# Another order of the attention stage in a two-layer encoder kernel

## The chip, the cores and the metric

One core of a Trainium2 chip. The metric is the device time of the whole program in microseconds (us), here the median of three runs. Engines are called TensorE (PE in the profile, its weight loads PEld), VectorE (DVE), ScalarE (ACT), GpSimd (POOL) and SyncE (SP).

## The reference

Two layers on x of 512 tokens by 1024 features, all in float32. Layer 0 mixes tokens by differential attention, layer 1 by a pooling mixer; each is followed by an MLP.

```python
h = rmsnorm(x, norm_mix[0])
q, k, v = split(h @ w_qkv)                 # 8 heads, two 64-wide maps each, v 128 wide
q = partial_rope(rmsnorm(q, q_gain)); k = partial_rope(rmsnorm(k, k_gain))
s = q @ k.T / sqrt(64)                     # 2 maps per head, 512 x 512
p = softmax(s); a = p[0] - lam * p[1]      # one learned lam
o = rmsnorm(a @ v, sub_gain) * (1 - lambda_init)
x = x + o @ w_o
x = x + square(relu(rmsnorm(x, norm_mlp[0]) @ w1[0])) @ w2[0]   # 1024 -> 4096 -> 1024
# layer 1: centred window means (2, 4, 8, 16) minus token, a matrix per group, then the same MLP
```

## The kernel before

Each float32 operand of a matmul is kept as a high and a low part (two tensors of the type fp32r), and a product is three matmuls: high by high, high by low, low by high (`three`). ScalarE makes the high part with a copy, VectorE the low part with a subtraction, so every tile that TensorE leaves in a PSUM bank is read by both, ScalarE first.

The attention has 8 heads of 4 query tiles, 32 tiles, treated as 16 pairs; pair j holds tiles 2j and 2j+1. The work is written out as steps j = 0 to 15 (and some more to drain), and each engine has its own program that follows the steps. Nothing is scheduled at run time: an engine does what is next in its program, and waits there for semaphores.

What TensorE does in step j: the scores of tiles 2j and 2j+1 (`scores`, into PSUM pairs 0 and 1, each a map per bank); the product of values and turned map of pair j-2 (`values`, bank 6); the transposes of the mixed maps of pair j-1 (`turn("map", ...)`, banks 4 and 5); then fillers, and side turns. A filler is work that doesn't belong to the pair, done in banks 6 and 7: fillers 0 to 7 project q and k of heads 4 to 7, 8 to 11 project v of these heads (24 matmuls each, in two parts of 12), and 12 to 19 are parts of the output projection w_o (6 to 18 matmuls). The table `FILL` says in which step and slot a filler's parts go. Side turns (`SIDE`) are transposes of q and k of the next head (even steps up to 12) and of a head's finished output (odd steps from 5), through banks 4 and 5, which they share with the map turns; `BACK` is the transpose of a head's values back to tokens (odd steps from 3, bank 4).

The others, for a tile or a pair: VectorE takes the negative maxima of a tile's scores (`maxima`, L1348); ScalarE the exponentials with their sums (`exps`, L969, two per tile); VectorE the reciprocal and the factor (`mix_root` L1353, `mix_factor` L1358) and `combine` (L1365), which subtracts lambda times the second map: this is called the mixing here. TensorE turns the map, ScalarE copies its high part (`keep_turn`, L913), VectorE its low part (`turn_lo`, L1310). A filler of q or k goes through ScalarE's copy and square (`qk_copy`, L894 and L897), VectorE's sum (`qk_sum`, L1272), GpSimd's root and product (`qk_root`, L690 and L696) and VectorE's rotation (`qk_norm`, L1292 to L1295). Side turns have the same two copies (L918, L1313). `o_stats` (L1371 to L1376) sums a head's squares. Weight slabs 4 to 8 (four pieces each) are split inside the steps by ScalarE (`split_hi`) and VectorE (`split_lo`) as the table `SPLIT` says; slab 8 is the first of the MLP's.

The order of the copies is each engine's own. Before, VectorE in step j does: the mixing of pair j-1, side turns of j-1, a v filler's low part, both maxima of j, the low halves of the map turns, sums of squares, weight pieces, q/k norms, head statistics. ScalarE: side copies and back copy of j-1, late fillers of j-1, exponentials of 2j, the map copies, exponentials of 2j+1, fillers, weight pieces. TensorE waits for the low half of a bank's last tile before it turns another into it (`turn`), and for the square of a filler's tile before it writes its bank again (`filler`).

After the steps come the rest of w_o, the sum with x per 128 features (`add_wo`, L1412), its squares and their sums on GpSimd (L733), the norm, and the MLP of layer 0.

## Time and profile before

| | us |
|---|---|
| median of three runs (990.47, 993.78, 994.23) | 993.78 |
| the profiled execution | 994.28 |
| its span, first to last instruction | 992.5 |
| TensorE busy in it | 967.6 |
| attention stage, steps 0 to 15 | 79.5 to 260.2 |

The profile shows one execution. Each engine's row of the timeline has the start and the length of an instruction, its line, its output and inputs; a bracket behind it gives the time that the engine was idle just before, and whose result ended that. Neighbouring equal instructions are drawn together (x8) and their lengths overlap, so the cost of one is the distance from its start to the next. The granted clock is the share of full speed that TensorE's clock was given in a stretch.

### The profile page before, as it was taken

The page shows a single profiled execution, that of the slowest core. Times are in us where ns is not written, and L with a number is a line of the kernel's source. Part 1 is how long each engine was busy: PE and PEld are TensorE (multiplying, and loading weights), DVE is VectorE, ACT ScalarE, POOL GpSimd, SP SyncE. Part 2 cuts the span into 40 slices and gives each one's busy share as a digit, 9 for nine tenths or more (in the row PEclk, how much of TensorE's full clock was granted, in tenths as well). Part 3 has the DMA queues.
Part 4 walks back from the last instruction along what each step waited for, and adds up shares of the span by engine and source line. Part 5 has one row for each costly group of instructions (what it writes and reads, how often), then busy time and mean ns, then how long its engine had stood idle before and what let it go on. Part 6 is the DMA issues. An engine that isn't in the chain of part 4 may idle for free.

```text
span 992.5 us, 12731 instructions
## 1 busy us (share of the span) xinstructions
PE 967.6 (97%) x4652; PEld 799.0 (81%) x4652; DVE 828.2 (83%) x1077; ACT 475.0 (48%) x743; POOL 351.5 (35%) x309
## 2 busy tenths in 40 slices
PE   8999898998999999999999999999999999999998
PEld 7887677877887878888888888988888888888887
DVE  5784877888566999999998888789998988989883
ACT  5645564667456452544534443575344353452520
POOL 6630333143346547385642200450431404314000
PEclk9999999999999999999999999999999999999999
DMA  7341211201140433333243232303333233322202
GB/s 260 89 126 43 86 43 43 85 1 44 43 153 34 131 108 105 108 104 109 86 124 96 79 129 82 128 1 106 107 106 106 86 111 101 122 91 85 86 0 85
DMA packets 50965, 90.12 MB, mean 91 GB/s; under 512 B 8268, under 2 KB 9560, under 8 KB 50904
## 3 DMA queue, kind: packets, MB, share of 16 engines
q1 hardware_dynamic: 45456, 89.14, 28.2%
q10 hardware_dynamic: 5448, 0.17, 0.3%
q8 instruction: 37, 0.61, 0.2%
q14 instruction: 24, 0.20, 0.1%
HBM read 87.20 MB, written 2.10 MB: 90 GB/s over the span
## 4 chain that ended last, share of the span: by engine, by line
PE 77%; DVE 13%; ACT 4%; POOL 3%; issue 2%; DMA 1%; SPq 0%; ACTq 0%; POOLq 0%; DVEq 0%
PE pair L1702 38%; PE bank L1702 36%; DVE s_nmax L1348 2%; DVE s_p L1365 1%; ACT s_p L969 1%; DVE s_w_lo L1199 1%; DVE s_aT_lo L1310 1%; POOL s_nsum L733 1%; POOL s_qk_r L690 1%; DVE s_acc L1467 1%; PE bank L1774 1%; DVE s_qkT_lo L1313 1%; ACT s_aT_hi L913 1%; DVE s_lbB_lo L1226 1%; DMA s_x_nat<-in_x 1%
## 5 line engine op out<-in xcount | busy, mean ns | idle before, releaser
L1226 DVE TENSOR_TENSOR s_lbB_lo<-s_lbB,s_b_hi 128x1024 fp32r<-128x1024 f32 x64 | 126.0, 1992 | 1.3 <-POOL s_lt L759 1.0
L759 POOL TENSOR_TENSOR s_lt<-s_lbB,s_lbB 128x1024 f32<-128x1024 f32 x14 | 34.7, 2476 | 260.4 <-PE pair L1702 162.4
L1199 DVE TENSOR_TENSOR s_w_lo<-s_raw,s_w_hi 128x1024 fp32r<-128x1024 f32 x72 | 118.9, 1675 | 3.1 <-ACT s_w_hi L838 3.1
L860 ACT ACTIVATE s_b_hi<-s_lbB 128x1024 fp32r<-128x1024 f32 x64 | 67.2, 1054 | 78.0 <-POOL s_lbB L759 35.5
L1702 PE MATMUL bank<-s_hT_hi,s_w_hi 128*128 128x512 f32 x256 | 100.2, 392 | 0.0
L1702 PE MATMUL pair<-s_hT_hi,s_w_hi 128*128 128x512 f32 x256 | 100.2, 391 | 0.0
L1702 PE MATMUL bank<-s_hT_hi,s_w_lo 128*128 128x512 f32 x256 | 99.6, 389 | 0.0
L1702 PE MATMUL bank<-s_hT_lo,s_w_hi 128*128 128x512 f32 x256 | 99.6, 389 | 0.0
L1702 PE MATMUL pair<-s_hT_hi,s_w_lo 128*128 128x512 f32 x256 | 99.6, 389 | 0.0
L1702 PE MATMUL pair<-s_hT_lo,s_w_hi 128*128 128x512 f32 x256 | 99.6, 389 | 0.0
L1058 ACT ACTIVATE s_u_raw<-s_u_raw 128x512 f32<-128x512 f32 x64 | 40.4, 632 | 114.1 <-DVE s_u_raw L1434 114.1
L838 ACT ACTIVATE s_w_hi<-s_raw 128x1024 fp32r<-128x1024 f32 x60 | 61.6, 1052 | 42.1 <-PE pair L1702 20.1
L860 ACT ACTIVATE s_b_hi<-s_lt 128x1024 fp32r<-128x1024 f32 x42 | 44.6, 1061 | 73.1 <-POOL s_lt L759 64.3
L969 ACT ACTIVATE s_p<-pair,s_nmax 128x512 f32<-128x512 f32 x64 | 43.8, 698 | 43.4 <-DVE s_nmax L1348 43.4
L1470 DVE TENSOR_TENSOR s_acc<-s_acc,bank 128x512 f32<-128x512 f32 x84 | 55.1, 678 | 6.2 <-PE bank L1702 6.2
L690 POOL TENSOR_TENSOR s_qk_r<-s_qk_v,s_minus_half 128x8 f32<-128x8 f32 x16 | 30.2, 1889 | 84.4 <-DVE s_qk_v L1273 84.4
L1470 DVE TENSOR_TENSOR s_acc<-s_acc,pair 128x512 f32<-128x512 f32 x84 | 55.1, 679 | 4.3 <-PE pair L1702 4.3
L1702 PE MATMUL bank<-s_b_hi,s_u_hi 128*128 128x512 f32 x144 | 56.6, 393 | 1.1 <-DVE s_a_lo L1458 1.1
L1702 PE MATMUL pair<-s_b_hi,s_u_hi 128*128 128x512 f32 (+1 forms) x148 | 57.4, 388 | 0.0
L1702 PEld LDWEIGHTS pair<-s_hT_hi,s_w_hi 128*128 128x128 f32 x256 | 48.1, 188 | 10.4 <-DVE s_hT_lo L1416 0.4
L1702 PEld LDWEIGHTS pair<-s_hT_lo,s_w_hi 128*128 128x128 f32 x256 | 48.1, 188 | 10.2 <-issue 0.2
L1702 PEld LDWEIGHTS bank<-s_hT_lo,s_w_hi 128*128 128x128 f32 x256 | 48.1, 188 | 10.2 <-issue 0.2
(272 smaller groups left out, 2664.0 us busy)
## 6 DMA issues: line engine op xcount, KB each, us to landing
s_raw<-in_mlp_w SPq DMA_DIRECT2D x64, 512.0 KB, 3.7
s_lbB<-in_mlp_w SPq DMA_DIRECT2D x64, 512.0 KB, 3.3
s_raw<-in_attn_w_qkv SPq DMA_DIRECT2D x24, 512.0 KB, 4.5
s_raw<-in_attn_w_o SPq DMA_DIRECT2D x8, 512.0 KB, 3.3
s_x_nat<-in_x SPq DMA_DIRECT2D x4, 512.0 KB, 7.1
out<-s_acc SPq DMA_DIRECT2D x7, 256.0 KB, 2.0
s_raw<-in_pool_w SPq DMA_DIRECT2D x4, 256.0 KB, 2.7
out<-s_acc SPq DMA_DIRECT2D x2, 128.0 KB, 1.9
```

Source lines behind the costliest of these rows:

```text
L690: root = g.tensor_tensor(qk_r[:, n % 2, :], qk_v[:, n % 2, :], minus_half[:], ALU.pow)
L733: g.tensor_tensor(nsum[:], first_sum, nsq[:, c % 4, :], ALU.add).then_inc(n_summed, 1)
L759: g.tensor_tensor(w2_raw[n][:], w2_raw[one][:], w2_raw[two][:], ALU.subtract).then_inc(t_done, 1)
L838: a.activation(w_hi[0][:, k * PIECE:(k + 1) * PIECE], raw[k][:], ACT.Copy).then_inc(w_hi_done, 1)
L860: a.activation(b_hi[home][:], w2_raw[n][:], ACT.Copy).then_inc(w2_hi_done, 1)
L969: a.activation(probs[n % 3][:, m, :], pair[n % 2][:, m, :], ACT.Exp, bias=nmax[:, n % 4, m:m + 1], accum_out=lsum[:, n, m:m + 1]).then_inc ...
L1058: a.activation(u_raw[:, f, :], u_raw[:, f, :], ACT.Square).then_inc(u_done, 1)
L1199: v.tensor_tensor(w_lo[slot][:, cols], raw[k][:], f32(w_hi[slot][:, cols]), ALU.subtract)\
L1226: v.tensor_tensor(w2_lo[n][:], w2_raw[n][:], f32(b_hi[home][:]), ALU.subtract).then_inc(w2_lo_done, 1)
L1348: v.tensor_reduce(nmax[:, n % 4, :], pair[n % 2][:], AX.X, ALU.max, negate=True).then_inc(max_done, 1)
L1470: last = v.tensor_tensor(dst, dst, src, ALU.add)
L1702: return nc.tensor.matmul(o, lhsT, rhs, start=start, stop=stop, **kw)
```

## The change

Four tables and orders are edited. A filler slot is added between the scores and the values (slot 0), so that the old slots 0 and 1 are now 1 and 2; filler 2 (step 1) and filler 5 (step 3) go into the new slot, ahead of the map turns, and of the others none follows another directly. On VectorE, the mixing of pair j moves from the start of step j+1 to step j, behind the low halves of the map turns; head statistics go ahead of those, side turns of step j and weight pieces behind the mixing. On ScalarE, side copies and the back copy move from the start of step j+1 to step j, ahead of the weight copies. The square of a q/k filler is taken from the copied tile and not from the bank, so TensorE waits for the copy only (`qk_copied`), and ScalarE waits for its own copy before the square. The last slab's pieces (slab 8) are split in steps 16 and 17 instead of 18 and 19.

```diff
-FILL = {(0, 0): ((0, 0), (0, 1)), (0, 1): ((1, 0), (1, 1)), (1, 0): ((2, 0), (2, 1)), (1, 1): ((3, 0),),
-        (2, 0): ((3, 1),), (2, 1): ((4, 0), (4, 1)), (3, 0): ((5, 0), (5, 1)), (3, 1): ((6, 0),),
-        (4, 0): ((6, 1),), (4, 1): ((7, 0), (7, 1))}
-FILL |= {(f - F_V + 5, 0): ((f, 0), (f, 1)) for f in range(F_V, F_Y)}
-FILL |= {(f - F_Y + 9, 0): ((f, 0),) for f in range(F_Y, F_END)}
+FILL = {(0, 1): ((0, 0), (0, 1)), (0, 2): ((1, 0), (1, 1)), (1, 0): ((2, 0), (2, 1)), (1, 1): ((3, 0),),
+        (2, 1): ((3, 1),), (2, 2): ((4, 0), (4, 1)), (3, 0): ((5, 0), (5, 1)), (3, 1): ((6, 0),),
+        (4, 1): ((6, 1),), (4, 2): ((7, 0), (7, 1))}
+FILL |= {(f - F_V + 5, 1): ((f, 0), (f, 1)) for f in range(F_V, F_Y)}
+FILL |= {(f - F_Y + 9, 1): ((f, 0),) for f in range(F_Y, F_END)}
...
-SPLIT = {4: (0, 0, 0, 1), 5: (2, 2, 3, 3), 6: (5, 5, 6, 6), 7: (10, 12, 13, 14), 8: (18, 18, 19, 19)}
+SPLIT = {4: (0, 0, 0, 1), 5: (2, 2, 3, 3), 6: (5, 5, 6, 6), 7: (10, 12, 13, 14), 8: (16, 16, 17, 17)}
...
-                a.activation(qs[n % 4][:], src[:], ACT.Copy, scale=in_r[:, n % NT:n % NT + 1])
+                a.activation(qs[n % 4][:], src[:], ACT.Copy, scale=in_r[:, n % NT:n % NT + 1]).then_inc(qk_copied, 1)
+                act.wait_ge(qk_copied, n + 1)
                 if n >= 3:
                     act.wait_ge(qk_v_done, n - 2)
-                a.activation(qsq[n % 3][:], src[:], ACT.Square, scale=in_r[:, n % NT:n % NT + 1])\
-                    .then_inc(qk_squared, 1)
+                a.activation(qsq[n % 3][:], qs[n % 4][:], ACT.Square).then_inc(qk_squared, 1)
...
             for j in range(END + 1):
-                for turn in SIDE.get(j - 1, ()) if j else ():
-                    keep_turn(*turn)
-                if j - 1 in BACK:
-                    keep_back(BACK[j - 1])
                 for f in range(F_END):
-                    if FILLED[f] == (j - 1, 1) or F_V <= f < F_Y and FILLED[f] == (j - 1, 0):
+                    if FILLED[f] == (j - 1, 2) or F_V <= f < F_Y and FILLED[f] == (j - 1, 1):
                         filled(f)
                 if j < PAIRS:
                     exps(2 * j)
+                for f in range(F_END):
+                    if FILLED[f] == (j, 0):
+                        filled(f)
...
                 for f in range(F_END):
-                    if FILLED[f] == (j, 0) and not F_V <= f < F_Y:
+                    if FILLED[f] == (j, 1) and not F_V <= f < F_Y:
                         filled(f)
+                for turn in SIDE.get(j, ()):
+                    keep_turn(*turn)
+                if j in BACK:
+                    keep_back(BACK[j])
...
-            for j in range(END + 2):
-                if 1 <= j <= PAIRS:
-                    mix_root(j - 1)
-                    mix_factor(j - 1)
-                    combine(2 * j - 2)
-                    combine(2 * j - 1)
-                for turn in SIDE.get(j - 1, ()) if j else ():
-                    turn_lo(*turn)
+            for j in range(END + 1):
+                if j < PAIRS:
+                    maxima(2 * j)
                 for f in range(F_V, F_Y):
-                    if FILLED[f] == (j - 1, 0):
+                    if FILLED[f] == (j - 1, 1):
                         v_lo_part(1, f - F_V, bank[FILL_BANK[f]])
                 if j < PAIRS:
-                    maxima(2 * j)
                     maxima(2 * j + 1)
+                for f in range(F_V):
+                    if FILLED[f][0] == j - 1:
+                        qk_sum(2 * NT + f)
+                if j in STATS:
+                    o_stats(STATS[j])
                 if 1 <= j <= PAIRS:
                     turn_lo("map", 2 * j - 2)
                     turn_lo("map", 2 * j - 1)
-                for f in range(F_V):
-                    if FILLED[f][0] == j - 1:
-                        qk_sum(2 * NT + f)
+                if j < PAIRS:
+                    mix_root(j)
+                    mix_factor(j)
+                    combine(2 * j)
+                    combine(2 * j + 1)
                 for s, steps in SPLIT.items():
                     for k in range(4):
                         if steps[k] + 1 == j:
                             split_lo(s, k, s % 2)
+                for turn in SIDE.get(j, ()):
+                    turn_lo(*turn)
                 for f in range(F_V):
                     if FILLED[f][0] == j - 1:
                         qk_norm(2 * NT + f)
-                if j in STATS:
-                    o_stats(STATS[j])
...
             for j in range(PAIRS + 1):
                 if j < PAIRS:
                     scores(2 * j)
+                if 1 <= j < PAIRS:
+                    scores(2 * j + 1)
+                if j == PAIRS:
+                    pe.wait_ge(exp_done, 2 * STEPS)
+                    w_o_rest((0, 1, 2), (2, 3))
+                fillers(j, 0)
+                if j >= 2:
+                    values(j - 2)
                 if j:
-                    if j < PAIRS:
-                        scores(2 * j + 1)
-                    else:
-                        pe.wait_ge(exp_done, 2 * STEPS)
-                        w_o_rest((0, 1, 2), (2, 3))
-                    if j >= 2:
-                        values(j - 2)
                     turn("map", 2 * j - 2)
                     turn("map", 2 * j - 1)
-                fillers(j, 0)
+                fillers(j, 1)
...
-                fillers(j, 1)
+                fillers(j, 2)
```

In the waits of TensorE, `qk_squared` is replaced by `qk_copied` in five places, with the same counts.

## Rows read from the trace of the kernel before

**Rows 1.** The page: span and busy share of the engines.
```profile
span 992.5 us, 12731 instructions
...
PE 967.6 (97%) x4652; PEld 799.0 (81%) x4652; DVE 828.2 (83%) x1077; ACT 475.0 (48%) x743; POOL 351.5 (35%) x309
```

**Rows 2.** Windows: stretch, length, busy us of each engine, granted clock, DMA share, GB/s.
```profile
100.00:125.00 25.00, 20.87 (x99) 15.80 (x98) 21.42 (x42) 12.53 (x27) 9.35 (x6) 0.93 0.29 85
...
150.00:175.00 25.00, 22.20 (x121) 17.97 (x120) 17.81 (x38) 12.20 (x26) 8.45 (x7) 0.90 0.11 36
175.00:200.00 25.00, 25.00 (x143) 20.69 (x143) 21.85 (x36) 15.32 (x34) 3.35 (x3) 0.96 0.25 85
```

**Rows 3.** Waits of TensorE: who was waited for, us in all, times, longest.
```profile
PE bank L1774 <- DVE s_aT_lo L1310: 6.8, 5, 2.1
...
PE bank L1702 <- POOL s_nsum L733: 1.6, 1, 1.6
```

**Rows 4.** Timeline of TensorE, step 8: start, length, line, operation, output and inputs.
```profile
191.05 0.50 PE L1702 MATMUL pair<-s_qkT_hi 64*128 64x512 f32 x2
...
192.64 0.39 PE L1702 MATMUL bank<-s_aT_hi,s_val 128*128 128x256 f32 x1
...
194.19 1.03 PE L1774 MATMUL bank<-s_ident,s_p 128*128 128x128 f32 x8
...
194.98 0.47 PE L1702 MATMUL bank<-s_w_hi,s_hT_hi 128*128 128x512 f32 x1
...
200.53 1.03 PE L1774 MATMUL bank<-s_ident,s_qkn 128*128 128x128 f32 x8
...
201.50 0.50 PE L1702 MATMUL pair<-s_qkT_hi 64*128 64x512 f32 x2
```

**Rows 5.** Timeline of TensorE: starts of steps 1, 5 and 16, and two waits.
```profile
93.42 0.50 PE L1702 MATMUL pair<-s_qkT_hi 64*128 64x512 f32 x2
...
116.33 1.23 PE L1774 MATMUL bank<-s_ident,s_qkn 128*128 128x128 f32 x8 [0.58 <-DVE s_aT_lo L1310]
...
118.49 0.51 PE L1702 MATMUL bank<-s_w_hi,s_hT_hi 128*128 128x512 f32 x1 [0.94 <-ACT s_qsq L897]
...
153.64 0.50 PE L1702 MATMUL pair<-s_qkT_hi 64*128 64x512 f32 x2
...
260.17 0.71 PE L1702 MATMUL pair<-s_oT,s_w_hi 128*128 128x512 f32 x2
```

**Rows 6.** Timelines of ScalarE and VectorE: mixing of step 0, then weight halves, maxima.
```profile
88.31 0.69 ACT L969 ACTIVATE s_p<-pair,s_nmax 128x512 f32<-128x512 f32 x1 [4.63 <-DVE s_nmax L1348]
...
89.79 0.17 DVE L1353 RECIPROCAL s_rl<-s_lsum 128x2 f32<-128x2 f32 x1 [1.51 <-ACT s_p L969]
...
90.25 1.41 DVE L1365 SCALAR_TENSOR_TENSOR s_p<-s_p,s_mixc 128x512 f32<-128x512 f32 x2
...
102.53 4.84 DVE L1204 SCALAR_TENSOR_TENSOR s_w_lo<-s_raw,s_in_col,s_w_hi 128x512 fp32r<-128x512 f32 x6
...
112.21 2.35 DVE L1348 TENSOR_REDUCE s_nmax<-pair 128x2 f32<-128x1024 f32 x2
...
117.48 1.41 DVE L1204 SCALAR_TENSOR_TENSOR s_w_lo<-s_raw,s_in_col,s_w_hi 128x512 fp32r<-128x512 f32 x2
```

**Rows 7.** Timeline of ScalarE, step 11: map copies, then exponentials of the second tile.
```profile
223.49 1.09 ACT L913 ACTIVATE s_aT_hi<-bank 128x512 fp32r<-128x512 f32 x2
...
224.44 0.71 ACT L969 ACTIVATE s_p<-pair,s_nmax 128x512 f32<-128x512 f32 x1
```

**Rows 8.** Timeline of VectorE: maxima of steps 9, 15; weight piece, mixing; last pieces.
```profile
203.87 2.35 DVE L1348 TENSOR_REDUCE s_nmax<-pair 128x2 f32<-128x1024 f32 x2
...
225.33 1.22 DVE L1199 TENSOR_TENSOR s_w_lo<-s_raw,s_w_hi 128x1024 fp32r<-128x1024 f32 x1
...
226.46 0.16 DVE L1353 RECIPROCAL s_rl<-s_lsum 128x2 f32<-128x2 f32 x1
...
254.15 2.35 DVE L1348 TENSOR_REDUCE s_nmax<-pair 128x2 f32<-128x1024 f32 x2
...
284.06 4.62 DVE L1199 TENSOR_TENSOR s_w_lo<-s_raw,s_w_hi 128x1024 fp32r<-128x1024 f32 x4
```

More of the change, by code:

```diff
@@ L361, in build_trunk @@
         proj_done = sem("proj_done")
+        qk_copied = sem("qk_copied")
         qk_squared = sem("qk_squared")
@@ L1812, in _ @@
                 if tile >= 4:
-                    pe.wait_ge(qk_squared, tile - 3)
+                    pe.wait_ge(qk_copied, tile - 3)
                 project(tile, bank[tile % 4])
@@ L1843, in values @@
                 if p == 0:
-                    pe.wait_ge(qk_squared, 2 * NT + 2)
+                    pe.wait_ge(qk_copied, 2 * NT + 2)
                 if not late:
@@ L1862, in filler @@
                     if g == 1:
-                        pe.wait_ge(qk_squared, 2 * NT + 1)
+                        pe.wait_ge(qk_copied, 2 * NT + 1)
                     elif 1 < g < F_V:
-                        pe.wait_ge(qk_squared, 2 * NT + g + 1)
+                        pe.wait_ge(qk_copied, 2 * NT + g + 1)
                     elif F_V <= g < F_Y:
```

## The prediction

> **What bounds the kernel now.** I read the page's busy shares first, then the windows, then who waited for whom, then the timelines of the engines. TensorE is busy 97% of the span [rows 1], so the change can win only what it idles, some 25 us, and what its clock loses. The windows show where: in the attention stage (79 to 270 us) a stretch of 25 us has 20.9 or 22.2 us of TensorE in it, and there the granted clock falls below full speed, to 0.93, 0.90 and 0.96 of 2.4 GHz [rows 2], a mean over time at 2.4 and at 1.2. The waits say for whom: the low halves of the turned maps, 6.8 us, and once for the norm sums behind the attention, 1.6 us [rows 3]. The 14 holes in TensorE's timeline between 95 and 260 us (two of them in [rows 5]) come to 15.5 us. At the lost clock of [rows 2], 0.07 x 25 = 1.75 us and 0.10 x 25 + 0.04 x 25 = 3.5 us, some 4 us of work ran longer (part of the second stretch fell into a hole). So the attention could at best give back 19.5 us, the norm wait 1.6.
>
> **The change, part by part.** A step of a pair has fixed parts on TensorE. From step 8 [rows 4]: scores 1.6, values 1.55, map turns 0.8, a filler of 24 matmuls 5.55, side turns 0.97 us; a full step is 10.5 us.
>
> *Square from the copy.* ScalarE's 8 squares in the attention and 8 ahead of it read the copied tile and wait for the copy, about 0.2 us each (estimate: the copy's 0.7 us less the present distance of 0.6 us, and a semaphore). ScalarE has room, 12.5 of 25 us busy [rows 2]. TensorE's wait for the bank ends 0.6 us earlier. With that cover gone it would cost 0.2 us per filler.
>
> *Steps 0 to 2.* Step 1 begins at 93.42 in both kernels [rows 5]. Now filler 2 stands ahead of the map turns: 93.42 + 1.6 + 5.55 = 100.6. That fills the old holes there. But ScalarE's copy and square of filler 2 (1.45 us) stand ahead of the map copies (0.96, from 223.49 to 224.44 [rows 7]), and only then come the exponentials of the pair's second tile: 103.0. The mixing follows 1.48 us behind their start (88.31 to 89.79 [rows 6]) and takes 1.8 us (reciprocal and factor 0.4, two combines 1.4 [rows 6]): 106.3. Behind it, in VectorE's order, now stand three weight pieces and two q/k norms, and only then the maxima of step 2. The six weight halves took 4.84 us beside GpSimd's work, and two alone 1.41, a distance of 0.66 each [rows 6]; norms and mixing between them and the maxima took 112.21 - 102.53 - 4.84 = 4.84 us, 3.0 of it norms, of which I count 1.0 as GpSimd's disturbance. GpSimd is done by then in the new order, so I take 4.0 + 2.1: maxima at 112.4, against 112.21 before [rows 6]. Nothing is won: VectorE's work is the same, and it idled about 4 us while the map turns stood behind filler 2. Bounds: 112.4 and, at the disturbed prices, 114.2.
> TensorE meanwhile does scores, values, map turns and the rest of filler 3, without a hole, until 111.2. Then the side turn of q needs the bank of the map whose low half comes 4.1 us behind the maxima (112.21 to 116.33 [rows 6, 5]). So it starts at 116.5: one hole of 5.3 us in place of five of 0.6 to 1.4. Filler 4 starts at 118.15, against 118.49 [rows 5].
>
> *The clock in that hole.* Before, the clock fell at this place and cost 1.75 us; the second fall cost up to 3.5 [rows 2]. A single hole of 5.3 us is nearer to these places than to any that it survived (the waits of [rows 3], 2.1 us at the longest). I take 2.1 us for a fall, near the lower end since part of the 3.5 lay in a hole; bounds 0 and 3.5. Step 3 then begins at 118.15 + 5.55 + 2.1 = 125.8.
> The Trainium skill's page "TensorE: Matmul & The Clock Gate", section "Why this matters for your kernels", says to leave no long idle gap between bursts, or the array goes back to half clock; by it one long hole is worse than the several short ones that it replaces. The trace agrees only in part: its first fall came after holes of 1.4, 1.2, 0.6 and 0.9 us.
>
> *Steps 3 and 4.* The same again. Filler 5 ahead of values and map turns puts these at 125.8 + 1.6 + 5.55 + 1.55 = 134.5, the exponentials 1.5 us behind, the mixing from 137.5 to 139.3; two weight pieces and two norms (2.7 + 2.1) let VectorE go at 144.1. Step 4 begins on TensorE at 134.5 + 0.8 + 2.9 (half a filler) + 0.6 = 138.8. Its side turns need low halves from 144.1 + 4.1 and 0.7 for the head statistics that now stand ahead of them: 148.9. TensorE arrives at 138.8 + 1.6 + 1.55 + 0.8 + 2.85 = 145.6, a hole of 3.3 us where before there was none, and I take a fall of the clock here too, 2.1 us (bounds 0 and 3.5). Filler 7 follows at 150.0, and step 5 begins at 150.0 + 5.55 + 2.1 = 157.6, against 153.64 [rows 5]: 4.0 us later.
>
> *Steps 5 to 8.* Before, they took 201.50 - 153.64 = 47.9 us, holes and a slow clock within [rows 4, 5]. Now side copies come ahead of the weight copies, the mixing is done a step ahead, and each step is 10.5 us on TensorE. One wait is left: in step 6 the filler needs the value tile's low half, whose copy waits for the last q/k norms, which stand behind step 5's side turn on VectorE: 0.95 us. 4 x 10.5 + 0.95 = 42.9. Step 9 begins at 200.5, 1.0 us ahead. Bounds 42.0 and, with that stage's two old holes of 2.0 and 0.8 us back, 45.7.
>
> *Steps 9 to 15.* Here the fillers are short and TensorE waits for the loop of VectorE and ScalarE: maxima, exponentials, map copies, exponentials, mixing, side halves. The loop has the same links, cut at another place, so it isn't shorter. From maxima to maxima it took 254.15 - 203.87 = 50.3 us for six steps [rows 8]. A weight piece stood beside the exponentials: mixing would have begun at 224.44 + 1.48 = 225.9 and began at 226.46 [rows 7, 8], so it cost 0.55; now it stands behind the mixing and costs its whole 1.14. Three pieces: +1.8. The head statistics move into a gap ahead of the low halves and give back 0 to 0.86 us at each of three steps: -1.3. Sum +0.5, bounds -0.8 and +1.8. On the other side, VectorE enters step 9 in time, 1.3 us behind the scores instead of 203.87 - 201.50 = 2.4: -1.1. Step 16 began 6.0 us behind the last maxima (260.17 [rows 5, 8]) and does so again. Together -0.6.
>
> *Behind the attention.* Four weight pieces of 1.14 us (4.62 in all) stood between the last side half and the sums of layer 1 [rows 8]. Moved two steps ahead, into VectorE's idle time there, they let the norm chain begin 3 us earlier, and TensorE's 1.6 us of [rows 3] go. Bounds 0 and 1.6. VectorE idles for TensorE in the stretch after, so nothing is late next but TensorE itself.
>
> **Sum.** -1.0 (to step 9) - 0.6 - 1.6 = -3.2 us. The profiled execution took 994.28 us (span 992.5), 0.5 above the median of the runs, 993.78. 994.28 - 3.2 = 991.1 us; against the median -0.3%. About 0.5% (5 us) is what a measurement of this kernel can tell from no change.
>
> **Rivals.**
> *The clock stays up.* For it: holes of 2.0 and 2.1 us near 208 and 224 us left it at full speed. Against: two falls in the windows [rows 2], after less idle time in a row. It gives back 2 x 2.1 = 4.2 us: 986.9. The point: whether the stretch behind the hole at 111 us has a granted clock of 1.
> *VectorE isn't in the way.* If the norms and weight halves fall into waits instead of behind the mixing, both holes go: 5.3 + 3.3 and the clock's 4.2, less the part of 1.5 that other waits take back: about 980. Against it is the written order.
> *The cost of the disturbed halves, slower.* If GpSimd's roots again run beside VectorE's work behind the mixing, steps 1 and 3 each pay the prices of [rows 6]: +1.8 and +1.3. The holes grow to 7.1 and 4.6, the clock falls at 3.5 instead of 2.1 twice (+2.8), and the late norms carry a third fall into step 6 (+3.5). -3.2 + 9.4 = +6.2: 1000.5. It decides from a start of step 5 later than about 161 us. Against: by the new order GpSimd is done before those pieces begin.
> *It does nothing.* The waits only change their names, and the gain of steps 5 to 8 is eaten whole by steps 1 to 4 (step 5 some 1 to 3 us later still): 994.0.
>
> **Chances.** Forecast 0.42; clock stays up 0.18; VectorE not in the way 0.12; does nothing 0.13; slower 0.15. So faster by over 0.5%: 0.18 + 0.12 = 0.30; within 0.5%: 0.42 + 0.13 = 0.55; slower 0.15. The forecast's own range is 988 to 994.5 by the bounds on clock and tail. For 8 in 10 I reach into the cases beside it: 984.0, which leaves out the case at 980, to 997.5, which leaves out most of the slower one.
>
> **What would show it.** Right: in step 1 no hole in TensorE's timeline ahead of the map turns; one hole of about 5 us for a map's low half before the side turn of step 2, with VectorE in weight halves and norms until about 112; a second of about 3 us in step 4; step 5 starting near 157 to 158 and step 9 near 200; the granted clock under 1 twice before 160 us and at 1 from there to 200; waits of 1 to 2 us ahead of the side turns of steps 9, 11, 13, 15; no wait for the norm sums at 300 us. Wrong: no hole over 2 us in steps 2 and 4, a start of step 9 before 197 or after 203, or step 16 more than 59.5 us behind step 9.

## The result and the profile after

The changed kernel took 998.62 us (median), the kernel before 992.54 us in the same comparison: ratio 1.0063, 95% interval 1.0042 to 1.0085. It is slower by 0.6%, outside the predicted range of 984.0 to 997.5, on the side that had a chance of 0.15. A second comparison of the same code, e1_changed, gave 999.50 against 992.19 us, ratio 1.0069 (1.0054 to 1.0084). Of the five executions of the first comparison the profiled one was a disturbed one of 2365 us, so the trace read here is that of e1_changed. The execution traced there took 1001.64 us, the longest of its six, so its end is some 2 us later than the median's.

> The changed kernel itself, for a trace of it that can be laid beside that of before. Theory V (VectorE's work behind the mixing holds up the next step's maxima): holes of 4 us and more ahead of the side turns of steps 2 and 4, step 5 starting near 159 to 161 us against 153.6, and from there no more than 1 us lost up to step 16. Rival T (the tail's loop): step 5 near 157.6 as forecast, and 4 to 7 us lost in steps 9 to 15 by weight pieces behind the mixing. Rival C (clock): the holes are as forecast, 5.3 and 3.3 us, and the granted clock is under 1 for more than 8 us in all more than before. Time 998.5 us, 6 above the kernel before.

The page of the changed kernel, beside [rows 1]:

```profile
span 999.9 us, 12744 instructions
...
PE 969.4 (97%) x4652; PEld 801.3 (80%) x4652; DVE 836.2 (84%) x1077; ACT 475.8 (48%) x743; POOL 344.9 (34%) x309
```

The instruction counts of VectorE and TensorE are those of before, but VectorE is busy 8.0 us longer (836.2 against 828.2) and the span is 7.4 us longer. The same number of VectorE instructions took longer. That is the first hint; the shares (97% as before, and 84% against 83%) hardly give it.

Waits of TensorE (who was waited for, us in all, times, longest), beside [rows 3]:

```profile
PE bank L1779 <- DVE s_aT_lo L1314: 17.3, 7, 5.2
PE bank L1779 <- DVE s_qkT_lo L1317: 2.4, 2, 1.2
...
PE bank L1707 <- DVE s_val L1304: 1.4, 2, 1.1
...
PE bank L1779 <- POOL s_oc L711: 0.6, 1, 0.6
```

The wait for low halves of maps went from 6.8 to 17.3 us; the one for the norm sums is gone. The windows, beside [rows 2], show where the clock fell (ninth column, behind the busy times):

```profile
100.00:125.00 25.00, 19.82 (x96) 15.93 (x95) 19.21 (x38) 13.41 (x28) 6.32 (x5) 0.86 0.28 84
125.00:150.00 25.00, 21.52 (x126) 17.45 (x126) 16.51 (x33) 14.27 (x32) 7.07 (x6) 1.00 0.14 43
150.00:175.00 25.00, 23.88 (x133) 19.38 (x132) 20.77 (x41) 14.12 (x30) 8.53 (x7) 0.93 0.13 43
...
225.00:250.00 25.00, 20.17 (x134) 15.90 (x135) 21.25 (x31) 17.82 (x40) 7.93 (x6) 1.00 0.08 22
250.00:275.00 25.00, 21.11 (x119) 17.59 (x119) 19.17 (x27) 12.79 (x29) 9.98 (x8) 0.93 0.23 64
```

The timeline of TensorE, beside [rows 4, 5]: step 0, the two early holes with the fillers behind them, steps 3, 5 and 9, the last hole, and step 16:

```profile
80.03 0.51 PE L1707 MATMUL pair<-s_qkT_hi 64*128 64x512 f32 x2
...
117.21 1.94 PE L1779 MATMUL bank<-s_ident,s_qkn 128*128 128x128 f32 x8 [5.18 <-DVE s_aT_lo L1314]
118.81 0.79 PE L1707 MATMUL bank<-s_w_hi,s_hT_hi 128*128 128x512 f32 x1
...
126.50 0.50 PE L1707 MATMUL pair<-s_qkT_hi 64*128 64x512 f32 x2
...
149.69 1.56 PE L1779 MATMUL bank<-s_ident,s_qkn 128*128 128x128 f32 x8 [3.48 <-DVE s_aT_lo L1314]
150.90 0.78 PE L1707 MATMUL bank<-s_w_hi,s_hT_hi 128*128 128x512 f32 x1
...
157.95 0.50 PE L1707 MATMUL pair<-s_qkT_hi 64*128 64x512 f32 x2
...
201.73 0.50 PE L1707 MATMUL pair<-s_qkT_hi 64*128 64x512 f32 x2
...
266.41 1.03 PE L1779 MATMUL bank<-s_ident,s_oc 128*128 128x128 f32 x4 [3.20 <-DVE s_aT_lo L1314]
...
267.95 1.20 PE L1707 MATMUL pair<-s_oT,s_w_hi 128*128 128x512 f32 x2
```

Step 0 starts at 80.03 where before it started at 79.48, for reasons ahead of the change, so 0.55 us are taken off below. (In the traces of this study step 0 starts anywhere from 76.65 to 80.03 us; where two traces are compared further on, it is by distances between steps.)

| | before | forecast | measured, less 0.55 |
|---|---|---|---|
| side turn of step 2 | 116.33 | 116.5 | 116.66 |
| step 3 | 125.76 | 125.8 | 125.95 |
| side turn of step 4 | 146.47 | 148.9 | 149.14 |
| step 5 | 153.64 | 157.6 | 157.40 |
| step 9 | 201.50 | 200.5 | 201.18 |
| step 16 | 260.17 | 258.6 | 267.40 |
| end of the span | 992.5 | 989.3 | 999.35 |

Up to step 9 the forecast holds within 0.7 us. Between step 9 and step 16 the kernel loses 8.1 us more than forecast (66.2 us in place of 58.1), and behind step 16 another 1.2. So of the rivals in the expectation of e1_changed, T has the place right (step 5 as forecast, the loss in steps 9 to 15), V the two holes but not the start of step 5 or the quiet tail; C, too, has the holes, but by the windows from 100 to 275 us the clock's loss grew only from 5.25 to 7.0 us. T blames the weight pieces behind the mixing, which the next rows contradict.

The timeline of VectorE in that stretch, beside [rows 8]: maxima of step 9, statistics and mixing of step 10, mixing and weight piece of step 14, maxima of step 15:

```profile
203.44 1.22 DVE L1352 TENSOR_REDUCE s_nmax<-pair 128x2 f32<-128x1024 f32 x1
...
214.53 0.16 DVE L1380 SCALAR_TENSOR_TENSOR s_o_v<-s_o_ss,s_o_sq 128x4 f32<-128x4 f32 x1
...
217.03 3.38 DVE L1369 SCALAR_TENSOR_TENSOR s_p<-s_p,s_mixc 128x512 f32<-128x512 f32 x2
...
255.72 3.35 DVE L1369 SCALAR_TENSOR_TENSOR s_p<-s_p,s_mixc 128x512 f32<-128x512 f32 x2
259.00 2.30 DVE L1203 TENSOR_TENSOR s_w_lo<-s_raw,s_w_hi 128x1024 fp32r<-128x1024 f32 x1
261.22 2.34 DVE L1352 TENSOR_REDUCE s_nmax<-pair 128x2 f32<-128x1024 f32 x2
```

Maxima to maxima is 261.22 - 203.44 = 57.8 us; before it was 50.3 (51.3 in the traces of e3 and e4, which have the order of before here) and the forecast was 50.8. The excess of 7.0 over the forecast stands in four places: the pair of `combine` took 1.41 us before [rows 6] and here 3.38, 3.38 (at 236.38) and 3.35, 5.9 us more; the weight piece 2.30 instead of 1.22 [rows 8], 1.1 more. Each of these has GpSimd beside it; the weight pieces of steps 11 and 13, with no GpSimd beside them, took 1.22 us as before. GpSimd's timeline of step 10, and one line of step 14:

```profile
214.77 1.02 POOL L709 TENSOR_TENSOR s_o_r<-s_o_v,s_minus_half 128x4 f32<-128x4 f32 x1 [9.98 <-DVE s_o_v L1380]
215.86 1.04 POOL L711 TENSOR_TENSOR s_oc<-s_oc,s_o_r 128x512 f32<-128x512 f32 x1
216.86 1.31 POOL L720 TENSOR_TENSOR s_x_kept<-s_hT_hi,s_hT_lo 128x512 f32<-128x512 f32 x1
218.12 1.74 POOL L717 TENSOR_TENSOR s_y_part<-s_y_part,s_x_kept 128x512 f32<-128x512 f32 x1
219.83 1.72 POOL L720 TENSOR_TENSOR s_x_kept<-s_hT_hi,s_hT_lo 128x512 f32<-128x512 f32 x1
...
258.48 1.73 POOL L717 TENSOR_TENSOR s_y_part<-s_y_part,s_x_kept 128x512 f32<-128x512 f32 x1
```

The lengths read as taking turns. The first combine is issued at 217.03, while GpSimd's sum of 216.86 runs; that ends at 218.17. The first combine, taken by itself, is recorded until 218.71, 0.54 us behind that end, and GpSimd's sum of 218.12 is 0.45 us longer than its 1.29. It ends at 219.86, then the second combine has its turn and ends at 220.41, 0.55 us behind, and GpSimd's next is longer again. In the same way the weight piece of 259.00 is done 1.1 us behind the end (260.21) of the sum of 258.48. The Trainium skill's page "SBUF — State Buffer", section "Who interferes with whom", states this: a VectorE instruction with two inputs in SBUF and a GpSimd instruction that reads SBUF exclude each other, and the one issued later is blocked. The trace agrees: the combine (both maps) and the weight piece (raw and high part) have two such inputs and were slowed; the maxima, which read PSUM only, took 2.34 us as before, those at 241.00 beside a GpSimd sum (240.85, 1.27 us).

In the kernel before, the same two groups of work lay beside each other and VectorE lost nothing. VectorE and GpSimd there, at the mixing of pair 10:

```profile
217.18 0.16 DVE L1376 SCALAR_TENSOR_TENSOR s_o_v<-s_o_ss,s_o_sq 128x4 f32<-128x4 f32 x1
...
217.71 1.41 DVE L1365 SCALAR_TENSOR_TENSOR s_p<-s_p,s_mixc 128x512 f32<-128x512 f32 x2
```
```profile
217.42 1.02 POOL L708 TENSOR_TENSOR s_o_r<-s_o_v,s_minus_half 128x4 f32<-128x4 f32 x1 [11.90 <-DVE s_o_v L1376]
218.52 1.50 POOL L710 TENSOR_TENSOR s_oc<-s_oc,s_o_r 128x512 f32<-128x512 f32 x1
```

There the mixing followed the statistics by 0.53 us, so it ran beside GpSimd's root, and when the product came, the product waited (1.50 us instead of 1.04). The root, a tile of 128x4 that also comes from SBUF, began 0.29 us ahead of the combines and is recorded for 1.02 us, and yet didn't slow them (1.41 us for both): not every overlap in the records is a wait. The change puts the low halves and a wait for the exponentials between the two: 217.03 - 214.53 = 2.50 us, and by then GpSimd is in its long instructions and VectorE is the one that waits.

### The profile page after: what moved, and what is told of

Its sections match the earlier page's. It is cut to its first block, busy times and chain, and to the rows that moved or that the text cites. A ratio compares the mean times of both kernels' runs of the same rounds, so it can differ in the third digit from the quotient of the medians.

```text
span 2363.8 us, 12744 instructions
## 1 busy us (share of the span) xinstructions
PE 2358.9 (100%) x4652; PEld 1464.2 (62%) x4652; DVE 810.5 (34%) x1077; ACT 485.7 (21%) x743; POOL 305.4 (13%) x309
## 4 chain that ended last, share of the span: by engine, by line
PE 100%; DMA 0%; DVE 0%; issue 0%
PE pair L1707 48%; PE bank L1707 48%; PE bank L1779 3%; PE bank L1725 0%; PE bank L1787 0%; PE pair L2082 0%; PE bank L2094 0%; DMA s_x_nat<-in_x 0%; PE pair L2101 0%; PE pair L1793 0%; DVE s_acc L1701 0%; PE pair L1800 0%
## 5 line engine op out<-in xcount | busy, mean ns | idle before, releaser
L1707 PE MATMUL pair<-s_hT_hi,s_w_hi 128*128 128x512 f32 x256 | 213.4, 834 | 0.0
L1707 PE MATMUL pair<-s_hT_hi,s_w_lo 128*128 128x512 f32 x256 | 212.1, 829 | 0.0
L1707 PE MATMUL pair<-s_hT_lo,s_w_hi 128*128 128x512 f32 x256 | 212.0, 828 | 0.0
L1707 PE MATMUL bank<-s_hT_hi,s_w_hi 128*128 128x512 f32 x256 | 190.0, 742 | 0.0
L1707 PE MATMUL bank<-s_hT_lo,s_w_hi 128*128 128x512 f32 x256 | 188.0, 735 | 0.0
L1707 PE MATMUL bank<-s_hT_hi,s_w_lo 128*128 128x512 f32 x256 | 187.8, 734 | 0.0
L760 POOL TENSOR_TENSOR s_lt<-s_lbB,s_lbB 128x1024 f32<-128x1024 f32 x14 | 33.1, 2365 | 977.6 <-PE bank L1707 495.9
L1707 PEld LDWEIGHTS pair<-s_hT_hi,s_w_lo 128*128 128x128 f32 x256 | 90.0, 352 | 62.5 <-issue 62.4
L1707 PEld LDWEIGHTS pair<-s_hT_hi,s_w_hi 128*128 128x128 f32 x256 | 90.1, 352 | 62.3 <-issue 62.1
L1707 PE MATMUL bank<-s_b_hi,s_u_hi 128*128 128x512 f32 x144 | 117.0, 812 | 0.0
L1707 PEld LDWEIGHTS bank<-s_hT_hi,s_w_lo 128*128 128x128 f32 x256 | 81.8, 320 | 50.2 <-issue 48.2
L1707 PEld LDWEIGHTS bank<-s_hT_hi,s_w_hi 128*128 128x128 f32 x256 | 81.1, 317 | 50.4 <-issue 48.5
L1475 DVE TENSOR_TENSOR s_acc<-s_acc,bank 128x512 f32<-128x512 f32 x84 | 57.8, 688 | 155.0 <-PE bank L1707 155.0
```

The source lines that it names most:

```text
L760: g.tensor_tensor(w2_raw[n][:], w2_raw[one][:], w2_raw[two][:], ALU.subtract).then_inc(t_done, 1)
L1475: last = v.tensor_tensor(dst, dst, src, ALU.add)
L1707: return nc.tensor.matmul(o, lhsT, rhs, start=start, stop=stop, **kw)
```

## The experiments

Two theories were left for them. **Theory V:** the new slots of fillers 2 and 5 cost the early steps more than the rest of the change gives. **Theory G:** the head statistics, moved ahead of the low halves, let GpSimd loose beside the mixing. V was on record before the trace of e1_changed was read, G came out of it.

**e2_old_slots.** The changed kernel with two fillers back behind the map turns.

```diff
-FILL = {(0, 1): ((0, 0), (0, 1)), (0, 2): ((1, 0), (1, 1)), (1, 0): ((2, 0), (2, 1)), (1, 1): ((3, 0),),
-        (2, 1): ((3, 1),), (2, 2): ((4, 0), (4, 1)), (3, 0): ((5, 0), (5, 1)), (3, 1): ((6, 0),),
+FILL = {(0, 1): ((0, 0), (0, 1)), (0, 2): ((1, 0), (1, 1)), (1, 1): ((2, 0), (2, 1)), (1, 2): ((3, 0),),
+        (2, 1): ((3, 1),), (2, 2): ((4, 0), (4, 1)), (3, 1): ((5, 0), (5, 1)), (3, 2): ((6, 0),),
```

> The changed kernel with fillers 2 and 5 back behind the map turns, everything else of the change kept. Theory V: map turns of steps 1 and 3 come 5.5 us sooner, so VectorE mixes in the time that it idled, both holes shrink to under 1.5 us, and the time falls by 5 to 9 us, to 990 to 994. Rival T: it falls by less than 2 us, to 997 or more. Rival C: it falls by what the clock costs, 3 to 5 us.

Measured: 989.33 us, ratio to before 0.9971 (0.9958 to 0.9984), 10.2 us below the changed kernel by the medians and 9.7 by the ratios, a little more than the 5 to 9 expected. TensorE's timeline:

```profile
91.24 0.50 PE L1707 MATMUL pair<-s_qkT_hi 64*128 64x512 f32 x2
...
111.51 1.23 PE L1779 MATMUL bank<-s_ident,s_qkn 128*128 128x128 f32 x8 [1.47 <-DVE s_aT_lo L1314]
...
145.53 0.50 PE L1707 MATMUL pair<-s_qkT_hi 64*128 64x512 f32 x2
```

Steps 1 to 4 take 145.53 - 91.24 = 54.3 us. In the changed kernel they take 157.95 - 94.00 = 63.95, in the one before 60.2. The hole of 5.18 us is one of 1.47, the one of 3.48 is gone, and so are both falls of the clock before 250 us. So the two slots cost 9.7 us in these steps, as theory V has it; why they do is what e6 asks. The loop of steps 9 to 15 still takes 248.77 - 190.98 = 57.8 us from maxima to maxima, with three pairs of combines at 3.36 to 3.38 us, so what is lost there doesn't come from the slots. It also means that the other parts of the change gain 5.9 us there, which the forecast didn't see apart.

**e3_slab8_only** and **e4_copied_only.** The kernel before with one part of the change each: the last slab's pieces two steps sooner; the square from the copy.

```diff
-SPLIT = {..., 8: (18, 18, 19, 19)}
+SPLIT = {..., 8: (16, 16, 17, 17)}
```
```diff
-                a.activation(qs[n % 4][:], src[:], ACT.Copy, scale=in_r[:, n % NT:n % NT + 1])
+                a.activation(qs[n % 4][:], src[:], ACT.Copy, scale=in_r[:, n % NT:n % NT + 1]).then_inc(qk_copied, 1)
+                act.wait_ge(qk_copied, n + 1)
...
-                a.activation(qsq[n % 3][:], src[:], ACT.Square, scale=in_r[:, n % NT:n % NT + 1])\
-                    .then_inc(qk_squared, 1)
+                a.activation(qsq[n % 3][:], qs[n % 4][:], ACT.Square).then_inc(qk_squared, 1)
...
-                    pe.wait_ge(qk_squared, tile - 3)
+                    pe.wait_ge(qk_copied, tile - 3)
...
```

> The kernel before with nothing changed but that the last slab's four pieces are split in steps 16 and 17. All theories: the 1.6 us of waiting for the norm sums goes and the time falls by 1.6 us, ratio 0.998. If VectorE's lead is eaten later in layer 0's MLP, the wait is gone from the trace and the time is within 0.5 us of before.

> The kernel before with the square taken from the copied tile and TensorE released by the copy, nothing else. TensorE's four waits for the square, 3.7 us in all, shrink by 0.6 us each at the places where nothing else holds it: 1.2 to 2.4 us faster, ratio 0.998. If the self-wait on ScalarE costs more than 0.2 us each and is passed on to the mixing, it is 0 to 1.5 us slower instead.

Measured: e3 989.83 us, ratio 0.9976 (0.9967 to 0.9986), with no wait for the norm sums. By the ratio the slab's move alone is worth 2.4 us (1.4 to 3.3), which holds the forecast's 1.6. By the traces it is less: behind the start of step 16 e3 takes 731.3 us and the kernel before 732.3, and the other 1.9 us of difference lie in steps 0 to 15, where the two programs are the same. e4 992.40 us, ratio 1.0004 (0.9989 to 1.0019), nothing. Its waits of TensorE say why:

```profile
PE bank L1775 <- DVE s_p L1366: 4.4, 2, 2.6
PE bank L1703 <- ACT s_qs L895: 1.8, 4, 0.8
```

The wait for the tile fell from 3.7 us for the square to 1.8 for the copy, and the wait for the mixed map behind it grew from 3.3 to 4.4: VectorE was late anyway, so 1.1 of the 1.9 us won at one wait are paid back at the next.

**e5_stats_late.** The changed kernel with the head statistics behind the mixing.

```diff
-                if j in STATS:
-                    o_stats(STATS[j])
                 if 1 <= j <= PAIRS:
                     turn_lo("map", 2 * j - 2)
...
+                if j in STATS:
+                    o_stats(STATS[j])
                 for turn in SIDE.get(j, ()):
                     turn_lo(*turn)
```

> The changed kernel with one thing undone: the head statistics go back behind the mixing (and the weight piece), so that GpSimd's root, product and sums of x start behind VectorE's combines and not beside them. Theory G (two-input instructions of VectorE and GpSimd on SBUF hold each other up): the pair of combines in steps 10, 12 and 14 takes 1.4 us again instead of 3.4 and the weight piece of step 14 1.2 instead of 2.3, 7.0 us less; the statistics now stand in the loop, 2.6 us more. From the maxima of step 9 to those of step 15: 53.4 us instead of 57.8; time 4 to 6 us below the changed kernel. Rival W (the three weight pieces behind the mixing are what the tail lost): combines stay at 3.4 us or the loop stays at 57 us or more, and the time within 1 us.

Measured: 998.37 us, ratio 1.0059 (1.0041 to 1.0078), 1 us better and not the 4 to 6 expected, though the loop did what was expected: maxima of step 9 to those of step 15 take 251.82 - 198.41 = 53.4 us, and each pair of combines 1.41 or 1.42, so rival W falls. From step 0 to step 16 its trace has 181.7 us where the changed kernel's has 187.9, but behind step 16 it has 735.9 and not 732.0. A good part of the gain was lost there, at a place that the expectation hadn't looked at. TensorE before the last output turn:

```profile
284.26 0.92 PE L1779 MATMUL bank<-s_ident,s_oc 128*128 128x128 f32 x4 [2.78 <-POOL s_oc L711]
```

The last head's statistics now stood behind the weight pieces of the slab in step 18, so GpSimd's product came late, and the granted clock fell to 0.93 in the stretch from 275 to 300 us, where the changed kernel has 1.00.

**e10_stats18_first.** e5 with those last statistics first in their step.

```diff
+                if j in STATS and j >= PAIRS:
+                    o_stats(STATS[j])
...
-                if j in STATS:
+                if j in STATS and j < PAIRS:
                     o_stats(STATS[j])
```

> The changed kernel with its output statistics behind the mixing, as in e5_stats_late, but those of step 18 first in their step, ahead of the last weight's pieces. Both theories keep the loop at about 53.4 us. If the hole of 2.8 us ahead of the last output turn in e5 came from the place of step 18's statistics, it falls to about 0.6 us and the clock fall behind it (about 1.75 us) goes: about 4 us less than e5, 994 to 995. If the hole has another cause, it stays and the time is 998.

Measured: 994.24 us, ratio 1.0024 (1.0011 to 1.0037), 0.35% or 3.5 us below e5 by the ratios, near what was expected. The hole is 0.60 us:

```profile
282.78 0.66 PE L1781 MATMUL bank<-s_ident,s_oc 128*128 128x128 f32 x4 [0.60 <-POOL s_oc L711]
```

So moving the statistics in VectorE's order is worth 0.45% by the ratios, some 4.5 us, against the changed kernel. But in that order the statistics' own time (0.9 us a head) stands behind the mixing. It doesn't separate what GpSimd costs.

**e9_gpsimd_waits.** The changed kernel with one wait more, on GpSimd, and VectorE's order untouched. GpSimd's root, and with it all that follows on GpSimd, waits until the step's pair is mixed:

```diff
                 if j in STATS:
                     h = STATS[j]
+                    pool.wait_ge(a_done, min(2 * j + 2, STEPS))
                     pool.wait_ge(o_v_done, h + 1)
```

> The changed kernel with one wait more: GpSimd's root of the output statistics waits until VectorE has mixed the pair of that step, so that GpSimd's product and sums no longer run beside the mixing. VectorE's order is that of the changed kernel. Theory G (GpSimd's tensor operations slow VectorE's mixing): the pairs that took 3.35 to 3.38 us take 1.4 us again, maxima of step 9 to those of step 15 take 51 to 52 us instead of 57.8, and the whole 6 to 8 us less than the changed kernel, about 992 to 993. Rival (the moved statistics cost by standing ahead of the low halves on VectorE, whatever GpSimd does): mixing 1.4 us, but the loop stays above 56 us and the time within 2 us of the changed kernel. The piece of a weight's low half in step 14 may stay at 2.3 us under both.

Measured: 990.57 us, ratio to before 0.9985 (0.9971 to 0.9999). By the ratios that is 0.84%, some 8.3 us, below the changed kernel. VectorE's timeline, then GpSimd's:

```profile
200.86 1.22 DVE L1353 TENSOR_REDUCE s_nmax<-pair 128x2 f32<-128x1024 f32 x1
...
214.46 1.41 DVE L1370 SCALAR_TENSOR_TENSOR s_p<-s_p,s_mixc 128x512 f32<-128x512 f32 x2
...
251.69 2.34 DVE L1353 TENSOR_REDUCE s_nmax<-pair 128x2 f32<-128x1024 f32 x2
```
```profile
217.05 1.04 POOL L712 TENSOR_TENSOR s_oc<-s_oc,s_o_r 128x512 f32<-128x512 f32 x1
218.04 1.29 POOL L721 TENSOR_TENSOR s_x_kept<-s_hT_hi,s_hT_lo 128x512 f32<-128x512 f32 x1
219.29 1.29 POOL L718 TENSOR_TENSOR s_y_part<-s_y_part,s_x_kept 128x512 f32<-128x512 f32 x1
```

The combines take 1.41 us again, GpSimd's sums 1.29, and maxima to maxima is 251.69 - 200.86 = 50.8 us: the prediction's figure, and a little under the 51 to 52 expected here. Theory G stands, and its rival (the statistics cost by their place on VectorE) falls, since they are still in that place. The weight piece of step 14, too, takes 1.22 us.

**e6_weights_early.** The changed kernel with the weight pieces ahead of the head statistics and the low halves, to test what fills the early holes.

```diff
+                for s, steps in SPLIT.items():
+                    for k in range(4):
+                        if steps[k] + 1 == j:
+                            split_lo(s, k, s % 2)
                 if j in STATS:
                     o_stats(STATS[j])
                 if 1 <= j <= PAIRS:
                     turn_lo("map", 2 * j - 2)
...
                     combine(2 * j + 1)
-                for s, steps in SPLIT.items():
-                    for k in range(4):
-                        if steps[k] + 1 == j:
-                            split_lo(s, k, s % 2)
```

> The changed kernel with the weight pieces of VectorE ahead of the low halves of the map turns instead of behind the mixing; fillers 2 and 5 stay ahead of the map turns. Theory V (work behind the mixing holds the maxima up): the holes of steps 2 and 4, 5.2 and 3.5 us, shrink to 1.3 and 0.8 or so, since six and four weight halves then fill VectorE's idle time, the clock stays up there, and step 5 starts 8 to 10 us sooner, near 148 to 150. Time 6 to 10 us below the changed kernel. Rival F (any filler ahead of the map turns costs its own length, whatever VectorE does then): step 5 starts less than 3 us sooner.

Measured: 994.80 us, ratio 1.0028 (1.0014 to 1.0041), by the ratios some 4 us less than the changed kernel, under the 6 to 10 expected. The two early holes on TensorE:

```profile
112.82 1.63 PE L1779 MATMUL bank<-s_ident,s_qkn 128*128 128x128 f32 x8 [2.36 <-DVE s_aT_lo L1314]
...
145.16 1.09 PE L1779 MATMUL bank<-s_ident,s_qkn 128*128 128x128 f32 x4 [4.41 <-DVE s_aT_lo L1314]
```

The first shrank from 5.18 to 2.36 us: the maxima of step 2 come 29.07 us behind step 0 (107.61 - 78.54) and not 33.07, because three weight pieces now use the time in which VectorE waits for the map copies. The second grew from 3.48 to 4.41, since in step 4 VectorE has no such idle time and the low halves got four weight halves ahead of them. So step 3 comes 3.9 us sooner behind step 0, but step 5 only 2.0 (75.9 us against 77.9), not 8 to 10: that is the sign of rival F, under 3 us. The weight pieces behind the mixing explain about 4 of the 9.7 us that the slots cost, and only in steps 1 and 2; the rest goes with the place of the fillers, in a way that no run takes apart. The larger part of e6's gain lies elsewhere: steps 9 to 15 take 62.1 us instead of 66.2, with the weight pieces out of the way of the maxima and all at 1.21 us. The last slab's pieces stand ahead of the last statistics here, too, so it has e5's hole of 2.8 us as well.

**e7_slots_stats, e8_all_three, e11_slots_gpsimd, e12_slots_gpsimd_early.** Combinations: old slots with late statistics; the same with weight pieces early; old slots with GpSimd's wait; the same with weight pieces early. Their edits are those shown above, put together.

> Both undone: fillers 2 and 5 behind the map turns, statistics behind the mixing, the rest of the change kept. If the two losses add up: 989.3 less 4 to 6, so 983 to 985, and step 16 starts 8 to 9 us ahead of the kernel before. If the tail's loop takes up what the early steps win, 987 or more.

> As the one before, and the weight pieces ahead of the low halves of the map turns. Theory V: the weight pieces of steps 11, 13 and 15 leave the loop from maxima to maxima but push the low halves back by 0.2 to 1.1 us, and the early steps have no hole over 1 us: another 1 to 3 us less, 981 to 983. If it pushes the side turns back by the whole piece, it is the same or 1 us slower than the one before.

> The changed kernel with fillers 2 and 5 in their old slots and GpSimd's wait of e9. If the two costs are separate, they add: 989.3 less 6 to 7, 982 to 984. If they share a cause (the later start of the loop over steps 9 to 15), less than that: 986 to 989.

> e11 with the pieces of the weights' low halves ahead of the low halves of the steps, behind statistics and mixing. In the early steps as in e6: maxima of step 2 sooner by up to 4 us, of which the old slots leave little to gain, 1 to 2 us less than e11. Against it: a piece now stands beside GpSimd's product and sums and takes 2.3 instead of 1.2 us in the odd steps of the tail, 1 us each in up to three of them; then it is 1 to 2 us more than e11.

| | us | ratio to before, 95% interval |
|---|---|---|
| e7 | 988.08 | 0.9957 (0.9941 to 0.9974) |
| e8 | 985.19 | 0.9931 (0.9915 to 0.9948) |
| e11 | 981.17 | 0.9893 (0.9875 to 0.9911) |
| e12 | 983.44 | 0.9921 (0.9899 to 0.9942) |

e7 and e8 missed their expectations (983 to 985 and 981 to 983) by 3 and 2 us: both have the hole of 2.8 us of e5 ahead of the last output turn and take 734.8 and 735.1 us behind step 16. e11 is the fastest kernel of the study, 1.1% below the one before. The two costs add: by the ratios, 1.0069 less 0.0098 (e2) less 0.0084 (e9) is 0.9887, and it came to 0.9893. Its page and its longest wait:

```profile
span 979.2 us, 12752 instructions
```
```profile
PE bank L1780 <- DVE s_aT_lo L1315: 7.1, 6, 1.9
```

The low halves' wait is 7.1 us in place of 17.3, and the granted clock is 1.00 in every stretch of 25 us from 75 to 300 us. With the weight pieces early (e12) it is 2.3 us slower. Its expectation looked for 1 to 2 us more, from pieces that stand beside GpSimd in the tail. Two such pieces are there, one of 2.28 us at 211.88 and one of 2.07 at 229.81:

```profile
211.88 2.28 DVE L1204 TENSOR_TENSOR s_w_lo<-s_raw,s_w_hi 128x1024 fp32r<-128x1024 f32 x1
```

But from step 9 to step 16 e12 takes 58.3 us and e11 58.6, so they aren't what it lost. It won 1.0 us in steps 1 to 3 and lost 4.0 in step 4 (17.4 us instead of 13.4), where four weight halves now stand ahead of the low halves of the map turns, as in e6. TensorE waits for these, in e11 not at all, and the granted clock is 0.93 in the stretch from 125 to 150 us:

```profile
139.93 1.22 PE L1780 MATMUL bank<-s_ident,s_qkn 128*128 128x128 f32 x8 [2.28 <-DVE s_aT_lo L1315]
```

In e8, with the statistics behind the mixing, the same hole is 0.62 us, and early pieces are worth 2.9 us (988.08 to 985.19). So whether they help depends on what else stands ahead of the low halves.

## Why the prediction was wrong

*What bounds the kernel, the fixed parts of a step.* Right. TensorE's holes and its clock decide, and lost and won time both show in them.

*Steps 0 to 4.* Right, holes, clock and times. It put the hole of step 2 at 5.3 us (measured 5.18), that of step 4 at 3.3 (3.48), and step 5 at 157.6 (157.40). The clock fell at both, 0.86 and 0.93 in the windows. Filler 4 took 126.50 - 118.81 = 7.7 us, where in e2, at full clock, it took 5.66, and the side turn ahead of it 0.4 more: 2.4 us against the 2.1 taken. Filler 7 took 7.05, so 1.4 and 0.2 for its side turn, against 2.1. What it called "Nothing is won: VectorE's work is the same" was right of the kernel as changed, and e2 shows the price of the two slots at 9.7 us. (The 14 holes that it counts before the change are 13, with the same sum of 15.5 us.)

*Steps 5 to 8.* 43.8 us against 42.9. The wait for the value tile is there twice, 1.12 and 0.30 us, where one of 0.95 was forecast.

*Steps 9 to 15.* **This is the step that failed**: "The head statistics move into a gap ahead of the low halves and give back 0 to 0.86 us at each of three steps: -1.3", with "Sum +0.5, bounds -0.8 and +1.8". The loop lost 7.5 us. The statistics did fit into the gap, but they are what GpSimd waits for, and GpSimd's five instructions, from 214.77 to 221.55 in step 10, moved with them, onto the mixing. Their price was taken as nothing, without a word. With GpSimd held back (e9) the loop takes 50.8 us, the forecast of the term to a tenth, so its other parts were sound. The bound was wrong by that one omission: three pairs of disturbed combines and a disturbed weight piece. [rows 6], with a weight half at 0.8 us beside GpSimd and 0.66 alone, could have shown that there was something to price, but at their rate, a fifth, the 5.45 us of these instructions would have grown by only 1.2 us (an estimate); the 7.0 had to be measured. The prediction had named the sign of this itself: step 16 more than 59.5 us behind step 9 (66.2 measured). Two smaller things add 1.1 us: VectorE enters step 9 1.7 us behind the scores, not 1.3, and step 16 starts 6.7 us behind the last maxima, not 6.0. With the 0.7 of step 9 and the loop's 7.0 that makes the 8.8 us of the table.

*Behind the attention.* -0.4 us instead of -1.6. The wait for the norm sums is gone, as said; e3 shows 1.0 us behind step 16 for that alone. But behind the hole of 3.20 us at 266.41 the first 12 matmuls of w_o ran to 271.88, 3.9 us instead of 3.0, at the fallen clock (0.93), and 0.6 us for the last head's product is new.

*The rivals.* The slower one had the right mechanism, GpSimd beside VectorE's instructions, and the wrong place: it looked for it behind the mixing of steps 1 and 3 and dismissed it there, rightly (in step 1 six weight halves took 4.06 us, undisturbed). The measured 998.6 us lies near its 1000.5, but by another way: step 5 started at 157.4, not after 161. The mechanism should have been asked of every step in which the trigger of GpSimd's work moves. The rival at 980, VectorE not in the way, did not happen; e11 comes to about its figure (981.17), but by undoing the slots and holding GpSimd back, so that is no proof of it. "The clock stays up" did not happen, "it does nothing" neither: large gains and larger losses came out at +0.6%.

One figure ahead of the prediction is wrong: TensorE's waits for `qk_squared` that became `qk_copied` are four lines, not five. Nothing rests on it.

## What to carry to other kernels

When an instruction moves, follow what it releases on the other engines, and put that work, too, at its new place in the timeline: here 0.9 us of VectorE's statistics moved into a free gap, and pulled 6.8 us of GpSimd's work onto the instructions that bound the loop. Where two engines exclude each other, the distance between the trigger and the bounding instruction decided who waits (0.53 us: GpSimd; 2.50 us: VectorE), and one more wait on the engine that has time, here GpSimd, was worth more (8.3 us, e9) than another order on the one that has none (4.5 us, e10). Such a wait doesn't show as idle time: the instruction is drawn longer, so compare the lengths of equal instructions. Split a change that has gains and losses: of this one the slots and the statistics cost 1.8% by the ratios, and the rest won 1.1%.

## What was not expected of the hardware

The lengths fit whole waits, in turns. Two combines of 0.67 us each took 3.38 us together, beside GpSimd sums of 1.29 us that took 1.72 to 1.74: each waits out the rest of the other's current instruction. One disturbed VectorE instruction of 1.22 us took 2.07 to 2.30.

The length of a hole alone didn't say whether the clock falls. In e9 a hole of 1.90 us at 222.31 was followed by scores that took 2.7 instead of 1.6 us (clock 0.95 and 0.98 in the stretches around it), while in e11 one of 1.91 us, at 212.63, left the clock at 1.00; in e10 one of 1.94 us at 257.71 by a fall to 0.93. In the changed kernel holes of 2.26 us at 226.85 and 1.59 at 246.19 left it at 1.00. The prediction's 2.1 us for a fall was close where it fell (2.4 and 1.6), but where it falls stays open, and no run was made for it. The Trainium skill's page "TensorE: Matmul & The Clock Gate", section "Why this matters for your kernels", which warns of long idle gaps, is borne out by the holes of 5.18, 3.48 and 3.20 us, each with a fall behind it; the falls behind 1.9 us are more than it says.
